# Two of sixteen dot products a unit moved from VectorE to TensorE, with their rows in buffers of their own; dots placed ahead of a top-k step's wait; first tile's matrix built in units 8 to 15

## The reference, cut to what matters

```python
q = (t @ peer_wq).reshape(T, 8, 2, 128)
sc = einsum('thpk,hpnk->thpn', q, peer_keys)        # 8 heads, 2 x 128 scores each
s_top, i_top = top_k(sc, 16)                        # both halves
cand = s_top[..., 0, :, None] + s_top[..., 1, None, :]
best_s, best_pos = top_k(cand.reshape(T, 8, 256), 16)   # 16 experts per head and token
g = softmax(best_s)
a = gelu(einsum('td,tkd->tk', xb, peer_u[eb]))      # 128 experts per token, rows of 2048
out = einsum('tk,tkd->td', g * a, peer_v[eb])
```

## Time and profile before

| what | value |
|---|---|
| median of 3 runs | 2490.89 us (2490.71 to 2491.93) |
| the profiled execution's own time | 2489.8 us |
| its span | 2487.9 us |
| mean granted TensorE clock | 0.855 |
| busy: PE, DVE, ACT, POOL | 71%, 67%, 32%, 41% of the span |
| mean HBM traffic | 271 GB/s |

### The profile page before, as it was taken

The page is one execution under the profiler, slowest core; times in us unless marked ns, Lnnn a source line. Parts: engine busy times, 40 slices in busy tenths (PEclk is TensorE's granted clock), DMA queues, the critical chain, the costliest instruction groups (busy, mean ns, idle before and its releaser), DMA issues.

```text
span 2487.9 us, 28481 instructions
## 1 busy us (share of the span) xinstructions
PE 1769.2 (71%) x9808; PEld 1451.7 (58%) x9808; DVE 1678.8 (67%) x2299; ACT 792.8 (32%) x1339; POOL 1011.9 (41%) x559
## 2 busy tenths in 40 slices
PE   7999999999999999999700000012112699999996
PEld 5888999998889888888700000011112566666663
DVE  5444455554445555557899999999999866666666
ACT  4444444344444444455300010256347600000000
POOL 0000000000000000001388888888878078888884
PEclk9999999999999999999955555555555999999998
DMA  5444465556555555546999999999999299999997
GB/s 163 131 141 145 137 189 184 185 172 196 189 187 185 186 186 187 185 150 239 354 342 352 353 356 349 348 362 344 355 360 423 75 385 411 411 409 411 411 412 292
DMA packets 217046, 674.87 MB, mean 271 GB/s; under 512 B 18784, under 2 KB 68320, under 8 KB 183520
## 3 DMA queue, kind: packets, MB, share of 16 engines
q0 software_dynamic: 57488, 393.25, 41.4%
q1 hardware_dynamic: 159456, 280.32, 33.8%
HBM read 671.42 MB, written 2.10 MB: 271 GB/s over the span
## 4 chain that ended last, share of the span: by engine, by line
PE 45%; DVE 27%; issue 15%; POOL 8%; DMA 3%; ACT 1%; DVEq 0%; POOLq 0%; ACTq 0%; SPq 0%
PE ps L413 44%; DVE junk L1545 18%; POOL v_rows L1751 7%; DMA v_rows<-in_v_gathered,idx_all 2%; POOL u_rows L1738 1%; DVE ohs L1568 1%; DMA u_rows<-in_peer_u,idx_all 1%; ACT hi L835 1%; DVE lo L1209 0%; DVE oh_k L1524 0%; DVE ohv L1528 0%; DVE ohs L1565 0%; PE ps L498 0%; DVE ij_all L1532 0%; DVE h L1583 0%
## 5 line engine op out<-in xcount | busy, mean ns | idle before, releaser
L1209 DVE TENSOR_TENSOR lo<-raw,hi 128x1024 fp32r<-128x1024 f32 x368 | 448.7, 1225 | 490.1 <-ACT hi L835 488.7
L1738 POOL DMA_INDIRECT u_rows<-in_peer_u,idx_all x256 | 597.9, 2336 | 198.6 <-issue 107.6
L1545 DVE SCALAR_TENSOR_TENSOR junk<-u_rows,h 128x2048 bf16<-128x2048 f32 x256 | 584.7, 2291 | 47.2 <-DVE best L1514 3.5
L835 ACT ACTIVATE hi<-raw 128x1024 fp32r<-128x1024 f32 x376 | 397.6, 1060 | 567.9 <-PE ps L413 565.5
L413 PE MATMUL ps<-v_raw,wt 128*128 128x368 f32 x1536 | 475.4, 472 | 2.8 <-DMA v_raw<-in_peer_v 2.0
L1751 POOL DMA_INDIRECT v_rows<-in_v_gathered,idx_all x256 | 391.1, 1528 | 151.4 <-issue 78.2
L413 PE MATMUL ps<-xh,hi 128*128 128x256 f32 (+2 forms) x1536 | 440.6, 287 | 2.6 <-ACT qkv L835 1.3
L413 PE MATMUL ps<-xh,lo 128*128 128x256 f32 (+2 forms) x1536 | 435.6, 284 | 0.0
L413 PE MATMUL ps<-xl,hi 128*128 128x256 f32 (+2 forms) x1536 | 435.0, 283 | 0.0
L1583 DVE SCALAR_TENSOR_TENSOR h<-v_rows,coef_all,h 128x944 f32<-128x944 f32 x256 | 307.6, 1201 | 172.9 <-DMA v_rows<-in_v_gathered,idx_all 171.9
L413 PEld LDWEIGHTS ps<-v_raw,wt 128*128 128x128 f32 x1536 | 291.7, 190 | 186.1 <-DMA v_raw<-in_peer_v 2.8
(11 more groups left out here) (217 smaller groups left out, 2271.7 us busy)
## 6 DMA issues: line engine op xcount, KB each, us to landing
raw<-in_w_in SPq DMA_DIRECT2D x96, 1024.0 KB, 5.4
v_raw<-in_peer_v SPq DMA_DIRECT2D x128, 552.0 KB, 7.8
raw<-in_w_in SPq DMA_DIRECT2D x64, 256.0 KB, 3.2
raw<-in_w_in SPq DMA_DIRECT2D x32, 512.0 KB, 4.6
raw<-in_p_a SPq DMA_DIRECT2D x16, 1024.0 KB, 5.0
raw<-in_p_b SPq DMA_DIRECT2D x16, 1024.0 KB, 5.1
raw<-in_w_o SPq DMA_DIRECT2D x16, 1024.0 KB, 5.1
raw<-in_peer_wq SPq DMA_DIRECT2D x16, 1024.0 KB, 6.7
```

The source lines that it names most:

```text
L835: return nc.scalar.activation(o, i, f, **kw)
L1209: V.tensor_tensor(raw_lo[:, hh // 2, k4, :] if kept else lo[:, hh % SLOT_N, :, :], raw[:, hh // 2, k4, :], (kept_hi(hh) if kept else hi[:, ...
L1545: V.scalar_tensor_tensor(junk[:, n % 2, :], u_rows[k % (RING if u else HEAD_RING)][:, :], 1.0, h1[:, u // PH, :], ALU.mult, ALU.mult, accu ...
L1738: Q.indirect_dma_start(u_rows[slot][:, :], None, peer_u, bass.IndirectOffsetOnAxis(ap=idx_all[:, n:n + 1], axis=0)).then_inc(u_in[slot], 16)
```

## The change

- **Two rows a unit go to TensorE.** In units 1 to 15, k = 0 and 1 (`PAIR`) are gathered into two buffers of their own (slots 6 and 7); the other 14 rows share a ring of 6. `dots_pair(u)` on PE transposes the two rows in 8 blocks (4 transposes of 128 x 128 each into PSUM), ACT copies each block of 128 x 512 to SBUF (`pair_copies`), and PE multiplies it by the transposed residual `h1t`: two float32 matmuls of 256 columns a block, accumulated in one bank. The dots are the diagonals of the result: DVE takes them with two instructions on 128 x 128 (`pair_dots`, multiply by the identity, sum along the row), as part 9 of the unit.
- **`h1t`** is made once for both tiles: 32 transposes on PE (`h1_turn`), 8 copies of 128 x 512 on ACT (`h1_copy`), before `gelu(0)`.
- **A dot stands between a step and its wait**: `chain.mark`, the dot, `chain.settle`.
- **All 15 parts** of a unit (14 dots and the pair) stand in the top-k; `coefs(u - 1)` stands behind part 8.
- **First tile's matrix**: four chunks a unit in each of units 8 to 15, behind that unit's `dots_pair` on PE and behind its `pair_copies`, `gelu(u - 1)` and `softmax_exp(u + 1)` on ACT; nothing of it is left behind unit 15.
- **Gathers of unit 1** are four of the ring, then the pair, then the rest. SP's panel 1 waits for the last products of the pair, since `h1t1` lies in its buffer.

```diff
+PAIR = (0, 1)
+PAIR_AFTER = 9
+ROW_RING = 6
+BLOCKS = KT // 2
+PER_UNIT = P // 4 // 8
...
     def link(self, ins):
+        self.mark(ins)
+        self.settle()
+
+    def mark(self, ins):
         ins.then_inc(self.sem, 1)
         self.k += 1
+
+    def settle(self):
         at = self.base + self.k
         self.eng.wait_ge(self.sem, at if self.i is None else self.i * self.per + at)
...
+            def dots_pair(u):
+
+                T, m = u // PH, u - 1
+                o = ps[:, 5 - 3 * (m % 2), 0:256]
+
+                def turn(b):
+                    g = m * BLOCKS + b
+                    if g >= 2:
+                        pe.wait_ge(S("ut_copied"), g - 1)
+                    for n in range(2):
+                        for r, k in enumerate(PAIR):
+                            kt = 2 * b + n
+                            last = nc.tensor.transpose(ps[:, 3 + g % 2, (2 * n + r) * P:(2 * n + r + 1) * P],
+                                                       u_rows[row_slot(u, k)][:, kt * P:(kt + 1) * P], ident[:, :])
+                    last.then_inc(S("ut_turned"), 1)
+
+                def products(b):
+                    g = m * BLOCKS + b
+                    pe.wait_ge(S("ut_copied"), g + 1)
+                    if b == 0 and m >= 2:
+                        pe.wait_ge(S("dots_done"), dot_place(u - 2, PAIR[1]))
+                    for n in range(2):
+                        kt = 2 * b + n
+                        last = mm(o, h1t[T][:, kt, :], ut[:, g % 2, n * 256:(n + 1) * 256], kt == 0, kt == KT - 1)
+                    last.then_inc(S("ut_used"), 1)
+
+                for k in PAIR:
+                    wait_row(pe, u, k)
+                turn(0)
+                for b in range(BLOCKS):
+                    if b + 1 < BLOCKS:
+                        turn(b + 1)
+                    products(b)
...
-            for u in range(PH, 2 * PH):
-                for half in range(2):
-                    if placed_half(u, half) >= 1:
-                        for c in range(2):
-                            place(2 * (placed_half(u, half) - 1) + c)
-            for c in range(2 * (2 * PH - 2), CHUNKS_T):
-                place(c)
+            h1_turn(0)
+            h1_turn(1)
+            for u in range(1, 2 * PH):
+                dots_pair(u)
+                if u == PH:
+                    slots_turn(0)
+                if u >= PH:
+                    for c in range((u - PH) * PER_UNIT, (u - PH + 1) * PER_UNIT):
+                        place(c)
...
+            def pair_copies(u):
+                for b in range(BLOCKS):
+                    g = (u - 1) * BLOCKS + b
+                    act.wait_ge(S("ut_turned"), g + 1)
+                    if g >= 2:
+                        act.wait_ge(S("ut_used"), g - 1)
+                    A(ut[:, g % 2, :], ps[:, 3 + g % 2, :], ACT.Copy).then_inc(S("ut_copied"), 1)
...
+            for T in range(NT):
+                h1_copy(T)
             gelu(0)
             softmax_exp(2)
-            for u in range(2, 2 * PH):
-                gelu(u - 1)
-                if u + 1 < 2 * PH:
+            for u in range(1, 2 * PH):
+                pair_copies(u)
+                if u > 1:
+                    gelu(u - 1)
+                if 3 <= u + 1 < 2 * PH:
                     softmax_exp(u + 1)
...
+                    for c in range((u - PH) * PER_UNIT, (u - PH + 1) * PER_UNIT):
+                        one_hots(c)
+                        if c % PER_UNIT:
+                            w_copy(c - 1)
+                    w_copy(c)
...
                 def step(ins):
-                    chain.link(ins)
-                    set_apart(dve)
+                    chain.mark(ins)
                     n = next(places)
                     if between and n in between:
                         between[n]()
+                    chain.settle()
+                    set_apart(dve)
...
+            def pair_dots(u):
+
+                m = u - 1
+                dve.wait_ge(S("ut_used"), (m + 1) * BLOCKS)
+                for r, k in enumerate(PAIR):
+                    bank = 5 - 3 * (m % 2)
+                    dve.wait_ge(S("dots_done"), dot_place(u, k) - 1)
+                    V.scalar_tensor_tensor(junk2[:, :], ps[:, bank, r * P:(r + 1) * P], 1.0, ident[:, :], ALU.mult, ALU.mult,
+                                           accum_out=dots[:, u % 2, k:k + 1]).then_inc(S("dots_done"), 1)
...
             def unit_part(u, n):
 
-                dot(u, n)
-                if n == 7 and u >= 2:
+                if n == PAIR_AFTER:
+                    pair_dots(u)
+                else:
+                    dot(u, n + 2 if n < PAIR_AFTER else n + 1)
+                if n == 8 and u > 1:
                     coefs(u - 1)
...
             def wait_free(u, k):
 
-                pool.wait_ge(S("dots_done"), dot_place(u, k))
+                if u == 0:
+                    if k >= HEAD_RING:
+                        pool.wait_ge(S("dots_done"), dot_place(0, k - HEAD_RING))
+                elif k in PAIR:
+                    if u > 1:
+                        pool.wait_ge(S("ut_turned"), (u - 1) * BLOCKS)
+                elif row_number(u, k) >= ROW_RING:
+                    before = row_number(u, k) - ROW_RING
+                    pool.wait_ge(S("dots_done"), dot_place(before // (TOPK - 2) + 1, before % (TOPK - 2) + 2))
```

More of the change, by code:

```diff
@@ L230, in decoder_layer @@
         iota = sb("iota", [P, P], F32)
+        junk2 = sb("junk2", [P, P], BF16)
         one = sb("one", [P, 1], F32)
@@ L765, in _, with h1_turn @@
             router_scores(3)
+            H1T_BANKS = (0, 1, 2, 6)
+            def h1_turn(T):
+                pe.wait_ge(S("h1_ready"), 4 * (T + 1))
+                for c, bank in enumerate(H1T_BANKS):
+                    if T:
+                        pe.wait_ge(S("h1t_copied"), c + 1)
+                    for n in range(4):
+                        kt = 4 * c + n
+                        last = nc.tensor.transpose(ps[:, bank, n * P:(n + 1) * P], h1[:, T, kt * P:(kt + 1) * P],
+                                                   ident[:, :])
+                    last.then_inc(S("h1t_turned"), 1)
             def tile_open(T):
@@ L1120, in gelu, with h1_copy @@
                 A(gel[:, u % 2, :], dots[:, u % 2, :], ACT.Gelu).then_inc(S("gelu_ready"), 1)
+            def h1_copy(T):
+                for c, bank in enumerate((0, 1, 2, 6)):
+                    act.wait_ge(S("h1t_turned"), 4 * T + c + 1)
+                    A(h1t[T][:, 4 * c:4 * c + 4, :].rearrange("p a t -> p (a t)"), ps[:, bank, :], ACT.Copy
+                      ).then_inc(S("h1t_copied"), 1)
+            def pair_copies(u):
[5 more added lines that the diff above has]
+                    A(ut[:, g % 2, :], ps[:, 3 + g % 2, :], ACT.Copy).then_inc(S("ut_copied"), 1)
             def slots_copy(T):
@@ L1610, in _ @@
             for u in range(1, 2 * PH):
-                parts = TOPK
+                parts = TOPK - 1
                 if u + 2 < 2 * PH:
-                    topk(u + 2, scores_of(u + 2), {n + 1: lambda n=n: unit_part(u, n) for n in range(min(parts, 15))})
-                    parts_done = min(parts, 15)
-                else:
-                    parts_done = 0
-                for n in range(parts_done, parts):
-                    unit_part(u, n)
+                    topk(u + 2, scores_of(u + 2), {n + 1: lambda n=n: unit_part(u, n) for n in range(parts)})
+                else:
+                    for n in range(parts):
+                        unit_part(u, n)
             coefs(2 * PH - 1)
@@ L1757, in _ @@
                 gather_u(0, k)
-            for u in range(1, 2 * PH):
+            indices(1)
+            for k in range(2, 2 + HEAD_RING):
+                gather_u(1, k)
+            pool.wait_ge(S("halves_used"), GROUPS * HALVES + HCRED)
+            pool.wait_ge(S("qk_done"), NT * 4)
+            for k in PAIR + tuple(range(2 + HEAD_RING, TOPK)):
+                gather_u(1, k)
+            for u in range(2, 2 * PH):
                 indices(u)
                 for k in range(TOPK):
-                    if u == 1 and k == HEAD_RING:
-                        pool.wait_ge(S("halves_used"), GROUPS * HALVES + HCRED)
-                        pool.wait_ge(S("qk_done"), NT * 4)
                     gather_u(u, k)
```

61 lines of the change are left out of this document (27 added, 34 removed).

## The result

The changed kernel takes 2399.07 us (median of 4 runs, 2398.14 to 2401.7) against 2491.41 us for the kernel before on the same chip: a ratio of 0.9631, 95% interval 0.9614 to 0.9648, so 92 us less. The forecast was 2415 us, with a range of 2390 to 2466. The direction and the range held; the gain was 16 us larger than forecast, and the sum hides larger misses of both signs.

A forecast was written before the change was run, and what follows sets the result against it. DVE was taken to bound units 1 to 13, DMA just below; 2489.8 us, less 73.6 (units 1 to 13), less 2 (units 14 and 15), plus 1.5 (before gelu(0)), less 1 (behind the last dot) gave 2415 us, range 2390 to 2466.

The forecast's parts named there:

- Waits of the steps: Top-k units: a dot ahead of each step's wait removes 0.21 us for 15 dots, 3.2 us a unit.
- Two dots fewer: DVE in top-k units: 4.4 us a unit off, 0.8 us added for the pair's two instructions.
- DMA: Top-k units: the same 16 row blocks need 39.7 us, 0.9 below DVE's 40.6, so hidden with almost nothing over.
- The gathers: POOL in top-k units: one gather per running dot, one of 16 over; with the short ring 1.2 us added a unit.
- Units 14 and 15: Last units of dots, without top-k: DMA's rate decides, some 28 blocks left, 71.7 against 73.8 us, 2 us saved.
- ACT: Units 8 to 15: a round of 38.6 us fits under the 41.8 us unit, margin 1.6 us, cost nothing.
- Rival 1: Units 9 to 15: PE and ACT become the bound if the clock stays at 1.2 GHz; 2465 us, chance 0.09.
- Ahead: Before gelu(0): 32 transposes and 8 copies, some 6 us, make coefs(0) late; 1.5 us added.
- Behind: After the last dot: leftover placing and copies fall away, ACT's last round and slow PE records count against; 1 us saved.
- 2 (the 0.21 stays): Top-k units: the 0.21 us belongs to the change of instruction, not the wait; 41 us stay, 2456 us, chance 0.05.
- 3 (DMA at 353 GB/s): Row-dot units: DMA is the bound already, 47.5 us a unit; nothing gained, 2488 us, chance 0.03.
- Rival 4: Rows behind the pair, in a ring of 6: the first lands 9 us late each unit; slower, 2517 us, chance 0.06.

The follow-up runs named there:

- experiment 1: Kernel before, with each dot put between a top-k step and its wait, all 16 dots left on DVE: 2433.42 us, ratio 0.9765.
- experiment 2: Changed kernel with the dot put behind the step's wait again, so only the pair on TensorE remains: 2444.73 us, ratio 0.9815.
- experiment 4: Changed kernel with row blocks of k = 8 to 15 in units 1 to 15 gathered at 4.4 KB a row, not 8 KB: 2390.54 us.
- experiment 5: Changed kernel with row blocks of k = 8 to 15 short (1104 columns) and their dots over 1024 columns alone: 2338.45 us.
- experiment 11: Changed kernel with unit 15's last two chunks placed behind the last dot and its four copies behind gelu(15): 2401.37 us, ratio 0.9634.
- experiment 6: Changed kernel with a ring of 5 row buffers, not 6: 2411.67 us.
- experiment 7: Changed kernel with a ring of 4 row buffers, not 6: 2475.23 us, 0.9937 of the kernel before.

## Why the prediction was right, and where it was not

**What bounds the kernel: right.** DVE before, DMA just below. Experiments 1 and 2 moved the unit by what they take off DVE: 42.8 and 43.9 us, where 43.1 and 43.8 were expected.

**Waits of the steps: right mechanism, term too small.** This is the term that made the total miss. "15 x 0.21 = 3.2 us a unit" measured 4.8, 0.32 a dot. The row showed the idle time before a dot; it did not show that the step's last instruction had 0.1 us to run which a dot can overlap. The back-to-back dots in the earlier trace rows say it, 2.21 us apart and 2.29 long, and the text quoted them for the wait alone. With it DVE's need is 39.0 us, not 40.6; 38.9 and 39.1 were found above.

**Two dots fewer: right.** 0.28 + 0.21 + 0.28 was to be 0.8 us; the instructions measured 0.28 and 0.29 and started 0.33 apart. The pair alone gave 3.7 us a unit, where 4.4 - 0.8 = 3.6 was stated.

**DMA: "hidden, with almost nothing over" was right for DVE at 40.6, and then not.** With DVE at 39 the bytes are a bound, and a unit's 16 blocks took 40.3 to 40.7 us and not 39.7: 413 to 418 GB/s over whole units, against the 421 of a short window that I divided by. (Even by that rate the sum was 0.2 short: 16.78 MB at 421 GB/s are 39.9 us.)

**The gathers: right mechanism.** A gather per dot, 0.94 us at the pair and in one gap opened by a waiting dot; this is the picture in the changed kernel and, with DMA relieved, in experiment 4. The addition was 1.2 us on 40.6. On 39 the unit's excess is 1.3, and DVE's waits for rows in units 1 to 13 sum to 15.2 us, 1.2 a unit. The 0.5 of it that was meant for the short ring is not borne out: POOL waited for no buffer. In the changed kernel itself bytes and gathers bound the unit at the same place, and how much of the wait is due to which is not separated; each alone suffices for it.

**Units 14 and 15: wrong, and with the wrong sign.** "DMA has some 28 blocks left ... saved: 2" supposed that two rows beside the pair were in when they began. They took 80.5 us, 32 blocks at 2.52: DMA was already full in unit 13, no stock was built up, and all 32 blocks had to come in that time. So 6.6 us were lost. Experiments 1 and 2 show the same sign, 78.5 and 78.3 us. A stretch that lives from a stock must be priced again when the stretch ahead of it no longer builds one.

**PE: right.** A pair was forecast at 13 us with the first one and a half blocks at 1.2 GHz. PE's timeline of unit 12's pair, from 1681.48 to 1694.57:

```profile
1681.48 1.94 PE L826 MATMUL ps<-ident,u_rows 128*128 128x128 f32 x8 [1.31 <-issue]
1683.26 2.07 PE L439 MATMUL ps<-ut,h1t 128*128 128x256 f32 x4
1685.12 1.06 PE L826 MATMUL ps<-ident,u_rows 128*128 128x128 f32 x4
1685.98 1.13 PE L439 MATMUL ps<-ut,h1t 128*128 128x256 f32 x4
1686.94 0.60 PE L826 MATMUL ps<-ident,u_rows 128*128 128x128 f32 x4
```

The first four product records last 2.07 us, the next four 1.13. The granted clock is 0.50 up to 1685.2 and 1.00 from 1687.0 on, and a block is 1.3 us from there on.

**ACT: right that it fits, the round too long by some 2 us.** The round was to be 38.6 us. One gelu follows the other by 37.0, 35.9, 38.9, 40.8 and 40.3 us from unit 9 on; the longer ones hold waits for late rows. The shortest, 35.9, is nearest to the round's own length, and experiment 5, where the round bounds, shows 36.3. The 38.9 of units 11 to 12, which looks like the forecast, is chance:

```profile
1655.84 0.22 ACT L911 ACTIVATE gel<-dots 128x16 f32<-128x16 f32 x1
...
1694.70 0.21 ACT L911 ACTIVATE gel<-dots 128x16 f32<-128x16 f32 x1
```

In unit 9 gelu(8) is done 21.9 us into the unit and wanted at 25.9, so the margin was 4 us, not 1.6. Rival 1 did not come: the clock did rise within each pair. Experiment 5 shows at which unit length this round bounds even so, some 36 us.

**Ahead: wrong, harmless.** 1.5 us were added for work before gelu(0). The coefficients waited 0.57 us for it, and DVE's stretch to unit 1 grew by 0.2; the projections ahead of it ended 1.5 us earlier in this execution, which is the -1.3 of the table.

**Behind: right in kind, too small.** 1 forecast, 1.9 in the profiles. The profile of experiment 11 shows both halves of the account, 5 us of leftovers against 2.5 us of a slower `tile_open`; its time can't be told from the changed kernel's.

**Rivals.** 2 (the 0.21 stays) and 3 (DMA at 353 GB/s) fell with experiment 1: a unit of 42.8 us at 389 GB/s. The Trainium skill (SBUF — State Buffer, "A bandwidth-pool intuition that's wrong") gives a core some 358 GB/s from HBM; the trace disagrees, with 413 GB/s over 524 us of the changed kernel. Rival 4, the short ring, was not met, but experiments 6 and 7 find its wait at one and two buffers less; even the ring of 4 is no loss against the kernel before.

The total came out 16 us under the forecast. The units gave 13 x (41.8 - 40.3) = 20 us more, and 2.2 of slip; nearly all of it is the waits of the steps, 1.6 us a unit too small. Units 14 and 15 took back 8.6. The rest, some 3 us, is the stretches ahead and behind. That the total lies so near is in part luck: two misses of opposite sign.

## What to carry to other kernels

Where a chain of dependent small instructions is interleaved with long independent ones, put the long one between a step and its wait, not behind the wait: here that alone gave 57 us, where the whole change gave 92. Work moved off the bounding engine pays only down to the next bound, so price what lies just below (here bytes, and gathers held up by the running dots) and every later stretch that lived from slack which the faster stage no longer leaves. An engine that is idle just ahead of a critical burst can be given work of that burst that is ready early; here TensorE's clock was up in time by it, with 3 us less to the first panel in the profile.

## What the runs showed of the hardware that was not expected

- A dot that needs nothing of the instruction ahead of it starts about 0.09 us before that one's recorded end (1657.01 against 1656.67 + 0.43), so a wait between the two costs 0.30 to 0.32 us and not the 0.21 of idle time that the trace shows.
- A gather that starts while a dot runs lasts 1.9 to 3.0 us, to some 0.8 us behind the dot's end (1643.51 + 2.83 against 1643.24 + 2.29). The one at 1668.56, 0.12 us ahead of the next dot, lasted 0.94: it had started first and was not held up. With dots of half the length on 8 of the 14, and more time without a dot, the mean gather fell from 2.10 to 1.40 us, by the page of each kernel.
- Gathers of 8 KB rows moved 413 to 418 GB/s over whole units and 421 in short windows. The DMA share was 0.99 already at 389 GB/s, so near the limit it told less than the rate.
